# Expert weights in wider column blocks: gate and up pieces of 1024 columns, inner chunks in pairs

## The chip, the cores and the metric

The kernel runs on one core of one Trainium2 chip. The metric is the device time of one execution in microseconds (us). TensorE does the matmuls, VectorE and ScalarE the element-wise work, GpSimd (POOL) some small work and its own transfers, and SyncE (SP) issues the weight transfers.

## The reference

The reference is a two-layer decoder trunk over 256 tokens of width 1024, in float32: a gated linear recurrence with a dense SwiGLU, then sparse attention with a mixture of eight experts of which each token takes two. The part that matters here is the last:

```
def swiglu(xn, w_gu, w_down):
    gate, up = jnp.split(xn @ w_gu, 2, axis=-1)
    return (jax.nn.silu(gate) * up) @ w_down

def moe_swiglu(xn, w_router, w_gu, w_down):
    logits = (xn @ w_router).astype(jnp.float32)
    vals, idx = lax.top_k(logits, TOP_K)
    wts = jax.nn.softmax(vals, axis=-1)
    combine = jnp.sum(jax.nn.one_hot(idx, N_EXPERTS, dtype=jnp.float32) * wts[..., None], axis=-2).astype(xn.dtype)
    out = jnp.zeros_like(xn)
    for e in range(N_EXPERTS):
        out = out + combine[..., e:e + 1] * swiglu(xn, w_gu[e], w_down[e])
    return out
```

Each expert has a gate and up matrix of 1024 x 7168 (3584 columns each) and a down matrix of 3584 x 1024, 42 MB in all.

## The kernel before

The recurrence, the dense layer and the attention come first and are not touched. The expert stage follows, from about 734 us on.

**Routing.** Every expert has up to 128 token rows (one block of 128 is worked on; a second pass is there for an expert with more, behind a test of the largest count). The rows of one expert are fetched from device memory (`x_rows`), transposed on TensorE (`turn_x`, bank 7 of PSUM) and split into a high and a low float32r part, `x_hi` and `x_lo` (`gathered`).

**Pieces.** The weights of an expert come in 42 pieces (`HALVES`) of 1 MB, each a tile of 128 x 2048. SyncE issues a transfer for each (`halves_of`, L472) into a ring of 7 raw slots (`RAWS`), and waits before each until VectorE has worked off the piece that was in the slot (`lo_ready`). ScalarE copies a piece to its high part `w_hi` (L776) and VectorE subtracts that from the raw data to get the low part `w_lo` (L1220). Both parts have 3 buffers (`PARTS`). TensorE gives one back with `w_free` after the last matmul of a piece. `split_to(n)` works the splits off up to piece n in the order of the program, so whatever else ScalarE or VectorE does stands between two splits.

**Products.** `product` (L1681) multiplies one piece with three terms: x_hi by w_hi, x_hi by w_lo, x_lo by w_hi. That is 12 matmuls of 128 x 128 by 512 columns a piece, 504 for an expert. For a gate or up piece (512 rows of the matrix by 512 columns, 2 KB a row) all 12 go to the same PSUM bank: four row blocks by three terms. For a down piece (256 rows by 1024 columns, 4 KB a row) they alternate between banks 5 and 6: two row blocks by three terms by two banks.

**Order.** The inner width of 3584 is cut into 7 chunks (`NCH`) of 512. For chunk c TensorE does the gate product (2 pieces) into bank 0 or 2, turns the hidden tile of chunk c-1 (4 transposes into bank 4, L1697), does the up product (2 pieces) into bank 1 or 3, and then the down product of chunk c-1 (2 pieces). ScalarE takes SiLU of the gate (L800, 128 x 512) when the gate product is done; VectorE multiplies it with the up product (L1270) to `m_h` and tells TensorE with `e_h`; ScalarE and VectorE make `t_hi` (L790) and `t_lo` (L1236) from the transposed tile. Banks, `m_sl`, `m_h`, `t_hi` and `t_lo` have two buffers each, by the parity of c. The order of pieces follows from `gu_item` and `down_item`. At the end of an expert `turn_x` of the next one stands among the last down pieces, ScalarE copies the result to `m_y` (L821, 128 x 1024), and GpSimd stores it.

**Last expert.** It is written out behind the loop. VectorE there also works out the routing shares (`shares`) and adds the results of the earlier experts to the output (`mix`, L1257, four times 128 x 1024).

Of the kernel before, what the change touches and what calls it, by code (L numbers as in the profile page):

```python
# [41 lines left out]
FF, FFE, NE = 2816, 3584, 8  # L42
# [94 lines left out]
def trunk(nc, x, norm_mix, norm_ffn, hgrn_w_in, hgrn_w_out, hgrn_g_norm, kv_norm, kv_w,  # L137
# [3 lines left out]
    with ExitStack() as ctx:  # L141
# [230 lines left out]

        def gu_item(c, half):
            return half if c == 0 else 3 * c - 1 + half

        def down_item(c):
            return 3 * c + 4 if c < NCH - 1 else PER_E - 1

        expert_items = sorted([(gu_item(c, g), "gate up".split()[g], c) for c in range(NCH) for g in range(2)]
                              + [(down_item(c), "down", c) for c in range(NCH)])

        def used(s, E):

            return w_free, E * HALVES + (s + 1 + PARTS)

        def part_of(s, w):

            return w[s % PARTS][:, :].rearrange("p (k c) -> p k c", c=D if expert_items[s // 2][1] == "down" else 512)  # L390

        def split_part(eng, s, E):

# [8 lines left out]
        def _(sp):  # L402
# [53 lines left out]
                load(columns(nsa_w_out[0], c * 512))  # L456
            assert i == I_MOE

            def halves_of(e, E, first, last):

                for s in range(first, last):
                    (_, kind, c), a = expert_items[s // 2], s % 2
                    if not (isinstance(E, int) and HALVES * E + s < RAWS):
                        sp.wait_ge(lo_ready, E * HALVES + (s - RAWS + 1))
                    if kind == "down":
                        src = moe_w_down[0, bass.ds(e, 1), c * 512 + a * 256:c * 512 + (a + 1) * 256, :]
                    else:
                        c0 = (kind == "up") * FFE + c * 512
                        src = moe_w_gu[0, bass.ds(e, 1), 512 * a:512 * a + 512, c0:c0 + 512]
                    src = src.rearrange("o (k p) c -> p (o k) c", p=P)  # L470
                    dst = raw[:, s % RAWS, :].rearrange("p (k c) -> p k c", c=D if kind == "down" else 512)
                    sp.dma_start(dst, src).then_inc(raw_full[s % RAWS], 16)  # L472

            def all_experts(E0):
# [119 lines left out]
        def _(act):  # L594
# [196 lines left out]

            def expert(e, E, q, last=False):
                ahead = 0 if last else PARTS - 1
                for c in range(NCH):
                    s = 2 * gu_item(c, 0) + 1
                    split_to(s + PARTS, E)
                    act.wait_ge(*used(s, E))
                    if c >= 2:
                        act.wait_ge(e_h, E * NCH + (c - 1))
                    act.activation(m_sl[:, c % 2, :], bank[:, 2 * (c % 2), :], ACT.Silu).then_inc(e_sl, 1)  # L800
                    if c:
                        hidden(c - 1, E)
                    if last and not q and c == 2:
                        split_to(2 * gu_item(2, 1) + 1 + PARTS, E)
                        act.wait_ge(PT_ps, 1)
                        act.activation(m_PT[:, :], bank[:, 7, 0:T], ACT.Copy).then_inc(PT_ready, 1)
                split_to(min(2 * gu_item(NCH - 1, 1) + 1 + PARTS, HALVES + ahead), E)
                if not last:
                    gathered(0, E + 1)
                split_to(min(2 * down_item(NCH - 2) + PARTS, HALVES + ahead), E)  # L810
# [34 lines left out]
        def _(dve):  # L845
# [413 lines left out]

            def expert(e, E, q, last=False):  # L1260
                ahead = 0 if last else PARTS - 1
                for c in range(NCH):
                    if c:
                        split_to(2 * gu_item(c, 0) + 1 + PARTS, E)
                        hidden(c - 1, E)
                    s = 2 * gu_item(c, 1) + 1
                    split_to(min(s + PARTS, HALVES + ahead), E)
                    dve.wait_ge(e_sl, E * NCH + (c + 1))
                    dve.wait_ge(*used(s, E))
                    dve.tensor_tensor(m_h[:, c % 2, :], m_sl[:, c % 2, :], bank[:, 2 * (c % 2) + 1, :],  # L1270
                                      ALU.mult).then_inc(e_h, 1)
                    if last and not q:
                        if c == 1:
                            shares()
                        if 2 <= c < 6:
                            tb, j = divmod(c - 2, 2)
                            dve.wait_ge(y_got[tb], 32)
                            step(mix(tb, j, m_mix))
                if not last:
                    gathered(0, E + 1)  # L1280
                split_to(min(2 * down_item(NCH - 2) + PARTS, HALVES + ahead), E)
# [35 lines left out]
        def _(pe):  # L1317
# [368 lines left out]
            def wide(c, up, E):  # L1686

                for a in range(2):
                    ks = range(4 * a, 4 * a + 4)
                    product([bank[:, 2 * (c % 2) + up, :]], 2 * gu_item(c, up) + a, E,  # L1690
                            [x_hi[:, k, :] for k in ks], [x_lo[:, k, :] for k in ks], 512, a == 0, a == 1)

            def turn(c, E):

                pe.wait_ge(e_h, E * NCH + (c + 1))
                for b in range(4):
                    last = tp(bank[:, 4, P * b:P * b + P], m_h[:, c % 2, P * b:P * b + P], ident)  # L1697
                last.then_inc(e_hT_ps, 1)

            def down(c, E, halves=(0, 1)):  # L1700
                pe.wait_ge(t_lo_ok, E * NCH + (c + 1))
                for a in halves:
                    bs = range(2 * a, 2 * a + 2)
                    product([bank[:, 5, :], bank[:, 6, :]], 2 * down_item(c) + a, E,
                            [t_hi[:, c % 2, b, :] for b in bs], [t_lo[:, c % 2, b, :] for b in bs], D,
                            c == 0 and a == 0, c == NCH - 1 and a == 1)

# [7 lines left out]

            def expert(e, E, q, last=False):
                pe.wait_ge(x_lo_ok, E * 2 + 2)
                for c in range(NCH):
                    if c >= 2:
                        pe.wait_ge(e_h, E * NCH + (c - 1))  # L1720
                    wide(c, 0, E)
                    if c:
                        if c > 1:
                            pe.wait_ge(t_lo_ok, E * NCH + (c - 1))
                        turn(c - 1, E)
                    wide(c, 1, E)
                    if c:
                        if c == 1:
                            pe.wait_ge(y_ready, E + (1 + q))
                        if last and not q and c == 2:  # L1730
# [4 lines left out]
                        if c < NCH - 1:  # L1735
                            down(c - 1, E)
# [55 lines left out]
```

## Time and profile before

| | us |
|---|---|
| median of 3 runs | 1725.07 (1723.33 to 1728.29) |
| profiled execution, its own time | 1724.83 |
| its span, first to last instruction | 1723.2 |
| mean granted TensorE clock over the span | 0.951 |
| TensorE busy over the span | 1612.6 (94%) |
| VectorE busy | 1145.4 (66%) |
| ScalarE busy | 934.5 (54%) |
| moved by the DMA engines | 455.56 MB, mean 264 GB/s |

The page cuts the span in 40 slices of 43 us. From slice 18 on, where the experts begin, the slices of TensorE and of the DMA engines are both at nine tenths or more; before that the DMA engines are mostly idle. Matmul ends are modelled, and matmuls overlap in the records: the distance between the starts of two matmuls is what tells their pace. A granted clock of 1.00 is 2.4 GHz, 0.5 is 1.2 GHz.

### The profile page before, as it was taken

The page shows a single profiled execution, that of the slowest core. Times are in us where ns is not written, and L with a number is a line of the kernel's source. Part 1 is how long each engine was busy: PE and PEld are TensorE (multiplying, and loading weights), DVE is VectorE, ACT ScalarE, POOL GpSimd, SP SyncE. Part 2 cuts the span into 40 slices and gives each one's busy share as a digit, 9 for nine tenths or more (in the row PEclk, how much of TensorE's full clock was granted, in tenths as well). Part 3 has the DMA queues.
Part 4 walks back from the last instruction along what each step waited for, and adds up shares of the span by engine and source line. Part 5 has one row for each costly group of instructions (what it writes and reads, how often), then busy time and mean ns, then how long its engine had stood idle before and what let it go on. Part 6 is the DMA issues. An engine that isn't in the chain of part 4 may idle for free.

```text
span 1723.2 us, 20000 instructions
## 1 busy us (share of the span) xinstructions
PE 1612.6 (94%) x7164; PEld 1253.3 (73%) x7164; DVE 1145.4 (66%) x1022; ACT 934.5 (54%) x906; POOL 56.8 (3%) x79
## 2 busy tenths in 40 slices
PE   6998899998976898799999999999999999999997
PEld 5866478876443786578878788788788788788775
DVE  1176245544022365378888888888888888888986
ACT  3323144433000132277777777877877877777774
POOL 2000000000001000100000000000000000000200
PEclk9999899999988578899999999999999999999999
DMA  9633235448464000099999999999999999999993
GB/s 364 218 99 98 69 127 195 171 146 215 157 234 170 1 1 1 28 354 376 353 390 374 349 385 367 364 380 363 370 382 365 366 369 360 383 366 352 399 384 126
DMA packets 212737, 455.56 MB, mean 264 GB/s; under 512 B 9825, under 2 KB 36490, under 8 KB 212682
## 3 DMA queue, kind: packets, MB, share of 16 engines
q1 hardware_dynamic: 206282, 440.97, 71.1%
q0 software_dynamic: 3536, 12.96, 1.9%
q10 hardware_dynamic: 2864, 0.90, 0.2%
q8 instruction: 33, 0.54, 0.1%
q14 instruction: 22, 0.18, 0.0%
HBM read 434.89 MB, written 19.92 MB: 264 GB/s over the span
## 4 chain that ended last, share of the span: by engine, by line
PE 87%; DVE 7%; ACT 2%; issue 2%; POOL 1%; DMA 0%; ACTq 0%; DVEq 0%; POOLq 0%
PE bank L1681 50%; PE bank L1439 11%; PE bank L1421 3%; PE bank L1362 3%; PE bank L1395 3%; PE bank L1489 3%; DVE w_lo L1220 2%; PE bank L1544 2%; PE bank L1384 2%; PE bank L1623 2%; PE bank L1597 1%; PE bank L1697 1%; ACT w_hi L776 1%; PE bank L1513 1%; POOL small L512 1%
## 5 line engine op out<-in xcount | busy, mean ns | idle before, releaser
L1220 DVE TENSOR_TENSOR w_lo<-ring,w_hi 128x2048 fp32r<-128x2048 f32 x336 | 764.2, 2291 | 131.6 <-ACT w_hi L776 131.1
L776 ACT ACTIVATE w_hi<-ring 128x2048 fp32r<-128x2048 f32 x336 | 643.4, 1920 | 181.7 <-PE bank L1681 178.8
L1681 PE MATMUL bank<-w_hi,x_hi 128*128 128x512 f32 x896 | 356.7, 398 | 14.9 <-DVE w_lo L1220 10.4
L1681 PE MATMUL bank<-w_hi,x_lo 128*128 128x512 f32 x896 | 350.4, 391 | 0.0
L1681 PE MATMUL bank<-w_lo,x_hi 128*128 128x512 f32 x896 | 350.2, 391 | 0.0
L1681 PEld LDWEIGHTS bank<-w_hi,x_hi 128*128 128x128 f32 x896 | 168.5, 188 | 55.6 <-DVE w_lo L1220 12.8
L1681 PEld LDWEIGHTS bank<-w_hi,x_lo 128*128 128x128 f32 x896 | 168.6, 188 | 36.8
L1681 PEld LDWEIGHTS bank<-w_lo,x_hi 128*128 128x128 f32 x896 | 168.9, 188 | 33.5
L1681 PE MATMUL bank<-w_hi,t_hi 128*128 128x512 f32 x448 | 143.0, 400 | 0.1
L952 DVE TENSOR_TENSOR ring_lo<-ring,f_whi 128x1024 fp32r<-128x1024 f32 x66 | 80.8, 1226 | 92.6 <-ACT f_whi L677 92.6
L1681 PE MATMUL bank<-w_lo,t_hi 128*128 128x512 f32 x448 | 141.2, 396 | 0.0
L1681 PE MATMUL bank<-w_hi,t_lo 128*128 128x512 f32 x448 | 141.0, 396 | 0.0
L677 ACT ACTIVATE f_whi<-ring 128x1024 fp32r<-128x1024 f32 x66 | 69.7, 1059 | 96.7 <-PE bank L1439 96.7
L1681 PEld LDWEIGHTS bank<-w_hi,t_lo 128*128 128x128 f32 x448 | 84.3, 188 | 20.5
L1681 PEld LDWEIGHTS bank<-w_lo,t_hi 128*128 128x128 f32 x448 | 84.4, 188 | 20.3
L1681 PEld LDWEIGHTS bank<-w_hi,t_hi 128*128 128x128 f32 x448 | 82.4, 188 | 21.3 <-DVE w_lo L1220 3.1
L1439 PE MATMUL bank<-f_whi,f_xhi 128*128 128x512 f32 x176 | 71.6, 407 | 4.2 <-DVE f_xlo L969 4.2
L1439 PE MATMUL bank<-f_whi,f_xlo 128*128 128x512 f32 x176 | 70.8, 402 | 0.0
L1439 PE MATMUL bank<-ring_lo,f_xhi 128*128 128x512 f32 x176 | 69.8, 397 | 0.0
L754 ACT ACTIVATE arena<-bank,small 128x128 f32<-128x128 f32 (+1 forms) x64 | 26.1, 419 | 61.4 <-DVE small L1153 61.4
L1362 PE MATMUL bank<-xT,ring 128*128 128x256 f32 x256 | 57.2, 387 | 2.2 <-DVE xT L861 2.2
L1362 PEld LDWEIGHTS bank<-xT,ring 128*128 128x128 f32 x256 | 49.7, 194 | 9.4 <-DVE xT L861 2.3
(251 smaller groups left out, 1631.1 us busy)
## 6 DMA issues: line engine op xcount, KB each, us to landing
ring<-in_moe_w_gu SPq DMA_DIRECT2D x224, 1024.0 KB, 7.2
ring<-in_moe_w_down SPq DMA_DIRECT2D x112, 1024.0 KB, 7.2
ring<-in_ffn_w_gu SPq DMA_DIRECT2D x22, 1024.0 KB, 6.7
ring<-in_hgrn_w_in SPq DMA_DIRECT2D x16, 1024.0 KB, 14.3
ring<-in_ffn_w_down SPq DMA_DIRECT2D x10, 1024.0 KB, 7.0
x_rows<-arena SPq DMA_DIRECT2D x2, 4096.0 KB, 21.1
ring<-in_kv_w SPq DMA_DIRECT2D x6, 1024.0 KB, 6.4
ring<-in_hgrn_w_out SPq DMA_DIRECT2D x4, 1024.0 KB, 8.1
```

Source lines behind the costliest of these rows:

```text
L677: act.activation(f_whi[d % F_PARTS][:, :], quarter(d)[0], ACT.Copy).then_inc(q_hi, 1)
L776: act.activation(w_hi[s % PARTS][:, :], raw[:, s % RAWS, :], ACT.Copy).then_inc(hi_ready, 1)
L952: dve.tensor_tensor(quarter(d)[1], quarter(d)[0], f_whi[d % F_PARTS][:, :].bitcast(F32), ALU.subtract).then_inc(q_lo, 1)
L1220: dve.tensor_tensor(w_lo[s % PARTS][:, :], raw[:, s % RAWS, :], w_hi[s % PARTS][:, :].bitcast(F32), ALU.subtract).then_inc(lo_ready, 1)
L1362: last = mm(bank[:, j % 4, 256 * hh:256 * hh + 256], cols(i)[:, k, c0:c0 + P], xT[:, k, :], start=k == 0, stop=k == KD - 1)
L1384: last = mm(bank[:, b, P * hh:P * hh + P], (a_kl if m > 1 else a_k)[:, hd, ts], (a_ql if m else a_q)[:, hd, ts], start=True, stop=True)
L1395: last = mm(bank[:, n % 4, :], xT[:, k, P * tb:P * tb + P], cols(4 + it)[:, k, :], start=k == 0, stop=k == KD - 1)
L1421: last = mm(bank[:, b0 + 2 * c + tb, :], lhs[:, k, P * tb:P * tb + P], cols(i0 + c)[:, k, :], start=k == 0, stop=k == KD - 1)
L1439: done = [mm(out_, x_, w_[:, k, 512 * b:512 * b + 512], start=start and n == 0, stop=stop and n == 2) for b, out_ in enumerate(dst)]
L1489: last = mm(bank[:, j % 4, :], b_xk[:, k, P * tb:P * tb + P], cols(I_KV + it)[:, k, :], start=k == 0, stop=k == KD - 1)
L1544: last = mm(bank[:, j, :], xT[:, k, P * tb:P * tb + P], cols(I_Q + it)[:, k, :], start=k == 0, stop=k == KD - 1)
L1681: last = mm(out_, x_[k], w[:, k, 512 * b:512 * b + 512], start=start and k == 0 and n == 0, stop=stop and k == HALF // width - 1 and n == 2)
```

## The change

The gate and up matrices are read in blocks of 1024 columns. The inner width now has four groups C (`WIDE`): three of 1024 columns (two chunks each) and one of 512. In a wide group a gate or up piece is 256 rows by 1024 columns (4 KB a row), so that a group has 4 gate pieces, into banks 0 and 1, and 4 up pieces, into banks 2 and 3. The last group keeps pieces of 512 rows by 512 columns, 2 of gate and 2 of up. The down pieces stay as they are. There are 42 pieces and 504 matmuls an expert, as before.

SiLU and the multiply work on both chunks of a group at once (128 x 1024). The banks and `m_sl`, `m_h` no longer alternate from group to group: a gate product of group C waits for the SiLU of group C-1 (`e_sl`), and the first turn of a group's hidden tiles waits for the multiply (`e_h`). The two chunks are turned between single gate pieces of the next group, and both down products follow its up product. The splits are ordered to match.

```diff
-PER_E = 3 * NCH
-HALVES = 2 * PER_E
+WIDE = 4
+HALVES = 6 * NCH
...
+        def pieces(C):
+            return 4 if C < WIDE - 1 else 2
+        def gate(C, a):
+            return (0, 8, 20, 32)[C] + a % pieces(C)
+        def up(C, a):
+            return gate(C, 0) + pieces(C) + a % pieces(C)
+        def down_half(c, a):
+            return (16, 18, 28, 30, 36, 38, 40)[c] + a
+        narrow = [f(WIDE - 1, a) for f in (gate, up) for a in range(2)]
...  SyncE
+            for C in range(WIDE):
+                n = pieces(C)
+                for a in range(n):
+                    rows, cols = slice(a * D // n, (a + 1) * D // n), slice(D * C, D * C + 256 * n)
+                    sources[gate(C, a)] = (moe_w_gu, rows, cols)
+                    sources[up(C, a)] = (moe_w_gu, rows, slice(FFE + cols.start, FFE + cols.stop))
...  ScalarE
+                for C in range(WIDE):
+                    if C:
+                        split_to(gate(C, 0) + PARTS, E)
+                        hidden(2 * C - 2, E)
+                    if 1 <= C < WIDE - 1:
+                        split_to(gate(C, 2) + PARTS, E)
+                        hidden(2 * C - 1, E)
+                    split_to(gate(C, -1) + PARTS, E)
+                    act.wait_ge(*used(gate(C, -1), E))
+                    if C:
+                        act.wait_ge(e_h, E * WIDE + C)
+                    n = pieces(C) // 2
+                    act.activation(m_sl[:, 0:n, :], bank[:, 0:n, :], ACT.Silu).then_inc(e_sl, 1)
...
+                split_to(up(WIDE - 1, 0) + PARTS, E)
+                hidden(NCH - 2, E)
...  VectorE
+                    split_to(up(C, -1) + PARTS, E)
+                    dve.wait_ge(e_sl, E * WIDE + (C + 1))
+                    dve.wait_ge(*used(up(C, -1), E))
+                    n = pieces(C) // 2
+                    dve.tensor_tensor(m_h[:, 0:n, :], m_sl[:, 0:n, :], bank[:, 2:2 + n, :], ALU.mult).then_inc(e_h, 1)
+                    if adds and C == 0:
+                        shares()
+                    if adds and C == 2:
+                        added(2)
...  TensorE
+            def wide(C, b0, s, a, E):
+                n = pieces(C)
+                ks = range(KD // n * a, KD // n * a + KD // n)
+                product([bank[:, b0 + b, :] for b in range(n // 2)], s, E,
+                        [x_hi[:, k, :] for k in ks], [x_lo[:, k, :] for k in ks], 256 * n, a == 0, a == n - 1)
             def turn(c, E):
-                pe.wait_ge(e_h, E * NCH + (c + 1))
+                pe.wait_ge(e_h, E * WIDE + (c // 2 + 1))
+                if c:
+                    pe.wait_ge(t_lo_ok, E * NCH + c)
...
+                for C in range(WIDE):
+                    if C:
+                        pe.wait_ge(e_sl, E * WIDE + C)
+                    for a in range(pieces(C)):
+                        wide(C, 0, gate(C, a), a, E)
+                        if C and a == 0:
+                            turn(2 * C - 2, E)
+                        if 1 <= C < WIDE - 1 and a == 2:
+                            turn(2 * C - 1, E)
+                    for a in range(pieces(C)):
+                        wide(C, 2, up(C, a), a, E)
+                        if C == WIDE - 1 and a == 0:
+                            turn(2 * C - 1, E)
...
+                    if 1 <= C < WIDE - 1:
+                        down(2 * C - 2, E)
+                        down(2 * C - 1, E)
+                down(NCH - 3, E, (0,))
                 if not last:
                     turn_x(0, E + 1)
+                down(NCH - 3, E, (1,))
                 down(NCH - 2, E, (0,))
                 turn(NCH - 1, E)
```

In the last expert VectorE does `shares` after the multiply of group 0, one addition after each turn's subtraction in group 2, one after its multiply and one at the start of group 3.

## Rows read from the trace of the kernel before

**Rows 1.** Busy time by engine, length of one expert; then clock, DMA share, GB/s.

```profile
core 0: us, PE busy (x) PEld busy (x) DVE busy (x) ACT busy (x) POOL busy (x), PEclk, DMA share, GB/s
...
1101.00:1223.00 122.00, 120.60 (x542) 98.12 (x541) 105.58 (x65) 92.97 (x68) 1.06 (x2) 1.00 1.01 370
```

**Rows 2.** Waits from 760 to 1600 us: total us, times, longest.

```profile
ACT w_hi L776 <- PE bank L1681: 149.3, 202, 1.0
DVE w_lo L1220 <- ACT w_hi L776: 112.1, 174, 3.2
...
PE bank L1681 <- DVE w_lo L1220: 8.1, 6, 1.4
```

**Rows 3.** Waits of SyncE's queue, same stretch.

```profile
SPq L472 <- DVE w_lo L1220: 661.4, 290, 4.9
```

**Rows 4.** The page's DMA issues: count, KB each, us to landing.

```profile
ring<-in_moe_w_gu SPq DMA_DIRECT2D x224, 1024.0 KB, 7.2
ring<-in_moe_w_down SPq DMA_DIRECT2D x112, 1024.0 KB, 7.2
```

**Rows 5.** Timeline of TensorE, a gate product's second piece and the turn behind it.

```profile
1010.55 0.39 PE L1681 MATMUL bank<-w_hi,x_lo 128*128 128x512 f32 x1
...
1013.27 0.40 PE L1681 MATMUL bank<-w_hi,x_lo 128*128 128x512 f32 x1
1013.50 0.60 PE L1697 MATMUL bank<-cf,arena 128*128 128x128 f32 x4
1013.86 0.48 PE L1681 MATMUL bank<-w_hi,x_hi 128*128 128x512 f32 x1
1014.17 0.39 PE L1681 MATMUL bank<-w_lo,x_hi 128*128 128x512 f32 x1
1014.40 0.39 PE L1681 MATMUL bank<-w_hi,x_lo 128*128 128x512 f32 x1
1014.63 0.40 PE L1681 MATMUL bank<-w_hi,x_hi 128*128 128x512 f32 x1
1014.87 0.39 PE L1681 MATMUL bank<-w_lo,x_hi 128*128 128x512 f32 x1
```

**Rows 6.** Timeline of TensorE, a down piece: first row and the thirteenth matmul.

```profile
1002.42 0.62 PE L1681 MATMUL bank<-w_hi,t_hi 128*128 128x512 f32 x2
...
1005.23 0.63 PE L1681 MATMUL bank<-w_hi,t_hi 128*128 128x512 f32 x2
```

**Rows 7.** Timeline, dense layer: gate and up, then down; twelve matmuls apart each.

```profile
270.78 0.39 PE L1439 MATMUL bank<-ring_lo,f_xhi 128*128 128x512 f32 x1
...
273.57 0.39 PE L1439 MATMUL bank<-ring_lo,f_xhi 128*128 128x512 f32 x1
...
396.69 0.63 PE L1439 MATMUL bank<-f_whi,f_hlo 128*128 128x512 f32 x2
...
399.50 0.63 PE L1439 MATMUL bank<-f_whi,f_hlo 128*128 128x512 f32 x2
```

**Rows 8.** Timeline of ScalarE at the start of an expert.

```profile
1222.46 1.03 ACT L821 ACTIVATE arena<-bank 128x1024 f32<-128x1024 f32 x1 [1.24 <-PE bank L1681]
...
1224.80 3.72 ACT L776 ACTIVATE w_hi<-ring 128x2048 fp32r<-128x2048 f32 x2
1228.54 1.28 ACT L800 ACT_TABLE_LOAD   x1
1229.83 0.60 ACT L800 ACTIVATE arena<-bank 128x512 f32<-128x512 f32 x1
```

**Rows 9.** Timeline of VectorE, same place.

```profile
1226.83 4.49 DVE L1220 TENSOR_TENSOR w_lo<-ring,w_hi 128x2048 fp32r<-128x2048 f32 x2 [3.18 <-ACT w_hi L776]
```

**Rows 10.** Instruction groups by line, 760 to 1600 us: busy us, mean ns.

```profile
L1220 DVE TENSOR_TENSOR w_lo<-ring,w_hi 128x2048 fp32r<-128x2048 f32 x291 | 662.6, 2291 | 112.1 <-ACT w_hi L776 112.1
L776 ACT ACTIVATE w_hi<-ring 128x2048 fp32r<-128x2048 f32 x291 | 557.3, 1920 | 149.4 <-PE bank L1681 149.3
...
L1270 DVE TENSOR_TENSOR arena<-arena,bank 128x512 f32<-128x512 f32 x48 | 32.7, 681 | 0.0
```

**Rows 11.** Timeline of TensorE: first matmul of two experts, third piece of the second.

```profile
1100.28 0.39 PE L1681 MATMUL bank<-w_hi,x_hi 128*128 128x512 f32 x1
...
1222.18 0.40 PE L1681 MATMUL bank<-w_hi,x_hi 128*128 128x512 f32 x1
...
1229.17 0.50 PE L1681 MATMUL bank<-w_hi,x_hi 128*128 128x512 f32 x1 [1.35 <-DVE w_lo L1220]
```

**Rows 12.** Timeline of VectorE in the last expert.

```profile
1630.87 1.28 DVE L1257 SCALAR_TENSOR_TENSOR h<-arena,h 128x1024 f32<-128x1024 f32 x1
```

More of the change, by code:

```diff
@@ L371, in left @@
             return res_ps, 8 + 2 * (i - I_OUT) + 2
[L375 to L382, printed above, removed]
+        def pieces(C):
[7 more added lines that the diff above has]
+        narrow = [f(WIDE - 1, a) for f in (gate, up) for a in range(2)]
         def used(s, E):
@@ L457, in _ @@
             assert i == I_MOE
+            sources = {}
+            for C in range(WIDE):
[4 more added lines that the diff above has]
+                    sources[up(C, a)] = (moe_w_gu, rows, slice(FFE + cols.start, FFE + cols.stop))
+            for c in range(NCH):
+                for a in range(2):
+                    sources[down_half(c, a)] = (moe_w_down, slice(512 * c + 256 * a, 512 * c + 256 * a + 256), slice(0, D))
             def halves_of(e, E, first, last):
                 for s in range(first, last):
-                    (_, kind, c), a = expert_items[s // 2], s % 2
+                    w, rows, cols = sources[s]
                     if not (isinstance(E, int) and HALVES * E + s < RAWS):
                         sp.wait_ge(lo_ready, E * HALVES + (s - RAWS + 1))
[L465 to L471, printed above, removed]
+                    src = w[0, bass.ds(e, 1), rows, cols].rearrange("o (k p) c -> p (o k) c", p=P)
+                    dst = raw[:, s % RAWS, :].rearrange("p (k c) -> p k c", c=512 if s in narrow else D)
                     sp.dma_start(dst, src).then_inc(raw_full[s % RAWS], 16)
@@ L793, in expert @@
                 ahead = 0 if last else PARTS - 1
[L794 to L804, printed above, removed]
+                for C in range(WIDE):
[11 more added lines that the diff above has]
+                    act.activation(m_sl[:, 0:n, :], bank[:, 0:n, :], ACT.Silu).then_inc(e_sl, 1)
+                    if last and not q and C == 1:
+                        split_to(up(1, -1) + PARTS, E)
                         act.wait_ge(PT_ps, 1)
                         act.activation(m_PT[:, :], bank[:, 7, 0:T], ACT.Copy).then_inc(PT_ready, 1)
-                split_to(min(2 * gu_item(NCH - 1, 1) + 1 + PARTS, HALVES + ahead), E)
+                split_to(up(WIDE - 1, 0) + PARTS, E)
+                hidden(NCH - 2, E)
+                split_to(down_half(NCH - 3, 0) + PARTS, E)
                 if not last:
                     gathered(0, E + 1)
-                split_to(min(2 * down_item(NCH - 2) + PARTS, HALVES + ahead), E)
+                split_to(down_half(NCH - 2, 0) + PARTS, E)
                 hidden(NCH - 1, E)
@@ L1261, in expert, with added @@
                 ahead = 0 if last else PARTS - 1
[L1262 to L1278, printed above, removed]
+                def added(n):
+                    tb, j = divmod(n, 2)
+                    dve.wait_ge(y_got[tb], 32)
+                    step(mix(tb, j, m_mix))
@@ new lines, in expert @@
+                adds = last and not q
+                for C in range(WIDE):
+                    if C:
+                        split_to(gate(C, 0) + PARTS, E)
+                        hidden(2 * C - 2, E)
+                        if adds and C == 2:
+                            added(0)
+                    if 1 <= C < WIDE - 1:
+                        split_to(gate(C, 2) + PARTS, E)
+                        hidden(2 * C - 1, E)
+                        if adds and C == 2:
+                            added(1)
+                    if C == WIDE - 1:
+                        if adds:
+                            added(3)
+                        split_to(up(C, 0) + PARTS, E)
+                        hidden(2 * C - 1, E)
+                    split_to(up(C, -1) + PARTS, E)
[5 more added lines that the diff above has]
+                        shares()
+                    if adds and C == 2:
+                        added(2)
@@ L1703, in down @@
                     bs = range(2 * a, 2 * a + 2)
-                    product([bank[:, 5, :], bank[:, 6, :]], 2 * down_item(c) + a, E,
+                    product([bank[:, 5, :], bank[:, 6, :]], down_half(c, a), E,
                             [t_hi[:, c % 2, b, :] for b in bs], [t_lo[:, c % 2, b, :] for b in bs], D,
@@ L1717, in expert @@
                 pe.wait_ge(x_lo_ok, E * 2 + 2)
[L1718 to L1730, printed above, removed]
+                for C in range(WIDE):
+                    if C:
+                        pe.wait_ge(e_sl, E * WIDE + C)
[9 more added lines that the diff above has]
+                            turn(2 * C - 1, E)
+                    if C == 1:
+                        if last and not q:
                             pe.wait_ge(PW_ready, 1)
```

14 lines of the change are left out of this document (5 added, 9 removed).

## The prediction

> **What bounds the kernel now.** I read the page's slices first (TensorE and the DMA engines are both full from 740 us to the end), then the busy times of one expert's stretch, the waits, and the timeline of single matmuls. In an expert's 122 us TensorE is busy 120.60 us, DMA share 1.01 at 370 GB/s, VectorE 105.58, ScalarE 92.97 [rows 1]. The waits decide between the two full ones: from 760 to 1600 us TensorE waited 8.1 us, in 6 places, always for a low part `w_lo`; ScalarE's splits waited for matmuls to give back a buffer and VectorE's for ScalarE; no one waited for a weight transfer [rows 2]. The queue that issues the transfers waited 661.4 us for VectorE to free a raw slot [rows 3]. A transfer lands 7.2 us after its issue [rows 4]; its slot's next use is seven pieces away, 7 x 2.72 = 19.0 us less the 4.2 us of a split, so some 7 us are spare. The expert stage is a stream of matmuls that the loads follow.
>
> Now its pace. A piece of weights (1 MB) is 12 matmuls. In a gate piece, all 12 into one bank, the starts lie 13.27 - 10.55 = 2.72 us apart [rows 5]; in a down piece, whose matmuls alternate between banks 5 and 6, 2.81 us [rows 6]. That is 227 against 234 ns a matmul, same shapes, clock 1.00. It is not the stationary tile alone: the dense layer's gate product (bank changed after every 3 matmuls) takes 2.79 for 12 and its down product (two banks in turn) 2.81 [rows 7], with other tiles in other places. Every product here that changes bank inside a piece runs at the slower pace.
>
> **The change part by part.**
>
> Transfers: 24 of an expert's 28 gate and up pieces become 256 rows by 4 KB instead of 512 by 2 KB. Bytes, count (336) and ring stay. Down pieces have 4 KB rows already and land in the same 7.2 us [rows 4], so little is to be had, and it would be hidden: 0.
>
> By the Trainium skill ("DMA: Bandwidth & Descriptors", Where 436 GB/s comes from) HBM binds such loads at about 358 GB/s. The trace's 370 [rows 1] is above that, and by the rule loads, at their ceiling whatever their rows, would set the pace; the waits say no. By it the time would stay near 1725, where case 4 below ends.
>
> Pace: a wide piece is now 2 row blocks x 3 products x 2 banks, the order of a down piece. I take it at 2.81 us: 24 x 0.09 = 2.16 us per expert. Bounds: 0 (pace stays 2.72) and 24 x 0.09. From this goes the settling that old pieces had after a bank change (the row after the transposes shows 0.31, 0.23, 0.23, 0.24 us for the first gaps, not 0.227 [rows 5]): some 0.02 to 0.05 us in 11 places, -0.2.
>
> The Trainium skill ("TensorE: Matmul & The Clock Gate", Back-to-back issue gap) lets the gap depend on the number of columns alone, about 216 ns at 512. The trace shows 227 and 234 at 512 columns, so the rule misses what I price; by it the pace term would be 0, which is case 2 below.
>
> Transposes: still seven turns of 4 an expert, each costing 0.36 us and a slow first gap (13.50 to 13.86, then 0.31) [rows 5]. They only move, from between gate and up to after single pieces: 0.
>
> Fewer, larger operations: per expert 4 SiLUs instead of 7 (three over 1024) and 4 multiplies instead of 7. A 1024-wide copy of ScalarE takes 1.03 [rows 8]. A multiply of 512 takes 0.68, at the rate of the 2048-wide subtraction (2.29) 1024 is about 1.2 [rows 10]. The fixed costs saved lie on engines that wait anyway: 0. But a long operation stands in front of a split. A split is 1.92 + 2.29 [rows 10] with about 0.3 of handing over (the low part starts 0.11 after the high one ends, TensorE 0.05 after it), 4.5 us from the freeing of a buffer, and the piece is due two pieces later: 5.62 us at the new pace, so 1.1 us of slack.
>
> Head of an expert, where the slack goes. Before: the output copy at 1222.46, a table load, then the splits of pieces 2 and 3 at 1224.80, a second table load at 1228.54, SiLU at 1229.83 [rows 8]; the first low part is made at 1226.83 [rows 9] and TensorE, which began the expert at 1222.18, starts piece 2 only at 1229.17 [rows 11]. The copy still stands ahead of split 2, so 1229.17 stays; pieces 0 and 1 are now 0.18 longer inside that wait: -0.18. Then, on the same clock: piece 3 starts at 32.07, 4 at 34.88, and 6 is due at 40.50. The split of 4 runs 28.5 to 30.4 (the table load and SiLU no longer ahead of it), that of 5 needs piece 2 done and ends at 34.2. Now the table load comes (to 35.5), SiLU of 1024 to 36.4, split 6 to 38.4, its low part 38.5 to 40.8: TensorE waits 0.3 us. The multiply of this pair must follow the last up piece (pieces 6 and 7 from 40.8, done at 46.5), but stands behind the low part of piece 9, whose buffer came free at 43.9 and which ends at 48.2; it ends at 49.4. TensorE does piece 8 till 49.3 and then turns, so it waits 0.1 us. Later pairs have down pieces in between for the low parts to catch up: 0. Head and handover: +0.4 - 0.2 = +0.2 us. Unfavourable bound: all six long operations (3 SiLUs, 3 multiplies) each expose 0.5 us, +3.
>
> Waits for single banks: `pe.wait_ge(e_sl)` ahead of a gate product is met one up product (11.2 us) after SiLU's input was ready; queued behind it would be all of TensorE. Banks 2 and 3 are guarded by the turn's `e_h`, bank 4 by the new `t_lo_ok` wait, two pieces (5.6 us) after the earlier turn, whose copy and subtraction take about 2 us: 0.
>
> Last expert: the routing shares (1.9 us of small operations) and four additions of 1.28 us on VectorE [rows 12] stand between subtractions before as after, with the slack of 1.1 us; I count them equal, with -1 as the favourable bound, since two of the additions now follow each other within wide pieces. There the output copy of an expert before is still ahead, so the same +2.2.
>
> Sum: 2.16 - 0.2 + 0.2 = 2.2 us per expert; x 8 = 17.3, less about 1 for the last. Rounded, +16.5. The profiled execution was 1724.8 us with a span of 1723.2, 1.6 us outside it, and the median 1725.07, 0.2 above it. So 1725 + 16.5 = 1741.5 us.
>
> **The rivals.** 0.3% (5.2 us) is about what a measurement of this kernel can tell from no change.
>
> 1. Pace and small waits as above: 1741.5. For it: three products out of three with bank changes are slow. Against: none is an `x_hi` product. Own range 1735 to 1748.
> 2. The pace stays 2.72 (it depends on the stationary tile, or is kept over a pair), but waits come. Pieces then are due earlier (slack 0.9), the head wait becomes 0.6, the handover 0.3 and two smaller of 0.1: about +1 per expert, 1733. For it: the `x` pieces settle to 227 within some matmuls of a disturbance.
> 3. The waits grow: slack is not regained between long operations, +3 us an expert on top of the pace: 1765. It decides once ScalarE and VectorE are over 2.81 us a piece for long. Against: VectorE has 105.58 of 122 us busy [rows 1], 0.4 us spare a piece.
> 4. No change: pace stays and the head's later SiLU is hidden: 1725 within 5. It needs both terms to fail.
> 5. Faster, the other side: the loads are the real pace and longer rows lift them. TensorE can gain no more than what it waits: 8.1 us in this stretch and about 2 beyond, so 1715. It decides if splits wait for data. Against: no such wait is in the trace [rows 2, 3], and the 4 KB transfers land no sooner than the 2 KB ones [rows 4].
>
> **How the numbers follow.** Chances: 0.60, 0.14, 0.10, 0.10, 0.06. The predicted time is that of case 1, 1741.5. The range of 8 in 10 takes in cases 1 and 2 and the near part of 3: 1731 to 1757. Slower by over 0.3% (above 1730): cases 1 and 3 and nearly all of 2, 0.83; within: case 4 and a little of 2, 0.11; faster 0.06.
>
> **What the profile after would show.** Right: wide gate and up pieces 2.80 to 2.82 us from start to start; an expert's first matmuls about 124.1 us apart instead of 121.9 [rows 11]; a wait of TensorE for `w_lo` at an expert's third and seventh piece; the second table load after four splits; fewer and larger packets, landing in 7 us or less, and still no wait for them. Wrong in the pace if the 12 starts stay within 2.72; wrong in the small waits if TensorE's waits for `w_lo` grow far over 2 us an expert, or if ScalarE is seen waiting for a transfer. What would overturn the whole: a matmul pace below 227 ns, which nothing in the trace offers.

## The result and the profile after

The changed kernel takes 1734.6 us (median of 22 runs) against 1724.4 for the kernel before (22 runs); the ratio is 1.0052, 95% interval 1.004 to 1.0064. It is slower by about 9 us by the ratio, 10.3 by the medians: outside 0.3%, and on the forecast side. One run of 1863.3, at a lower granted clock, is among the 22; the ratio leaves it out. The time lies in the range of 1731 to 1757 but beside the predicted 1741.5: it is that of case 2 (1733), whose chance was put at 0.14, and not of case 1.

The page and the views after, from the top. The page's first line, and its DMA part:

```profile
span 1733.7 us, 20010 instructions
...
DMA packets 163585, 455.56 MB, mean 263 GB/s; under 512 B 9825, under 2 KB 36490, under 8 KB 163530
...
ring<-in_moe_w_gu SPq DMA_DIRECT2D x224, 1024.0 KB, 7.3
ring<-in_moe_w_down SPq DMA_DIRECT2D x112, 1024.0 KB, 7.2
```

49,152 packets fewer than the 212,737 of before, and a gate or up piece lands 7.3 us after its issue, not sooner than [rows 4]. The change did what it says to the transfers, and no more came of it.

The same length of one expert as in [rows 1]:

```profile
core 0: us, PE busy (x) PEld busy (x) DVE busy (x) ACT busy (x) POOL busy (x), PEclk, DMA share, GB/s
...
980.00:1102.00 122.00, 120.11 (x538) 97.01 (x536) 103.98 (x61) 91.49 (x64) 1.06 (x2) 1.00 0.98 364
```

The clock is 1.00 as before. Every engine does a little less in 122 us: 538 matmuls instead of 542. How many fall into such a stretch depends on where it begins (536 from 978.8 us on), so the loss is not read from here but from the distance between two experts, below: 1.1%. The waits from 760 to 1600 us, beside [rows 2]:

```profile
ACT w_hi L791 <- PE bank L1718: 127.6, 151, 1.9
DVE w_lo L1241 <- ACT w_hi L791: 120.0, 158, 3.1
ACT t_hi L805 <- PE bank L1736: 59.7, 49, 1.6
...
PE bank L1718 <- DVE w_lo L1241: 10.6, 12, 1.3
```

TensorE waits 12 times for a low part instead of 6. This view counts as idle only what is left after the modelled end of the last matmul, so a stop of 0.3 us does not appear in it; starts show more. Nobody waits for a weight transfer. ScalarE's new 59.7 us is its place in the order: it stands at `t_hi` until a turn is done.

The pace, in TensorE's timeline, from the fourth piece of an expert, a wide gate piece, into the fifth (each row of x2 is two banks):

```profile
993.42 0.62 PE L1718 MATMUL bank<-w_hi,x_hi 128*128 128x512 f32 x2
993.87 0.62 PE L1718 MATMUL bank<-w_lo,x_hi 128*128 128x512 f32 x2
...
996.14 0.62 PE L1718 MATMUL bank<-w_hi,x_hi 128*128 128x512 f32 x2
```

996.14 - 993.42 is 2.72 us for 12 matmuls that change bank every time: the pace of [rows 5], not of [rows 6]. An expert, from its first matmul to the next one's, and the stop at its seventh piece:

```profile
982.21 0.40 PE L1718 MATMUL bank<-w_hi,x_hi 128*128 128x512 f32 x1
...
999.76 0.61 PE L1718 MATMUL bank<-w_hi,x_lo 128*128 128x512 f32 x2
1000.79 0.73 PE L1718 MATMUL bank<-w_hi,x_hi 128*128 128x512 f32 x2 [0.41 <-DVE w_lo L1241]
...
1008.63 0.61 PE L1718 MATMUL bank<-w_hi,x_lo 128*128 128x512 f32 x2
1009.37 0.66 PE L1736 MATMUL bank<-cf,arena 128*128 128x128 f32 x4
...
1105.44 0.63 PE L1718 MATMUL bank<-w_hi,x_hi 128*128 128x512 f32 x2
```

1105.44 - 982.21 is 123.23 us against 121.90 in [rows 11]: +1.33. By a stop I mean, from here on, what the distance between two starts has over that of a running stream. In a running stream the rows of two would follow each other by 0.45; 1.03 at the seventh piece is a stop of 0.58, and 0.74 ahead of the transposes one of 0.29 to 0.34 (the last matmul of a pair, 0.23 after its row, is followed by the transposes at 0.23 when nothing is late). ScalarE in that stretch, beside [rows 8]:

```profile
982.49 1.03 ACT L842 ACTIVATE arena<-bank 128x1024 f32<-128x1024 f32 x1 [1.14 <-PE bank L1718]
983.54 1.28 ACT L791 ACT_TABLE_LOAD   x1
984.83 5.52 ACT L791 ACTIVATE w_hi<-ring 128x2048 fp32r<-128x2048 f32 x3
992.25 1.92 ACT L791 ACTIVATE w_hi<-ring 128x2048 fp32r<-128x2048 f32 x1 [1.90 <-PE bank L1718]
994.19 1.28 ACT L821 ACT_TABLE_LOAD   x1
995.49 1.03 ACT L821 ACTIVATE arena<-bank 128x1024 f32<-128x1024 f32 x1
996.41 3.71 ACT L791 ACTIVATE w_hi<-ring 128x2048 fp32r<-128x2048 f32 x2
```

and VectorE:

```profile
998.45 6.70 DVE L1241 TENSOR_TENSOR w_lo<-ring,w_hi 128x2048 fp32r<-128x2048 f32 x3 [1.85 <-ACT w_hi L791]
1005.89 2.29 DVE L1241 TENSOR_TENSOR w_lo<-ring,w_hi 128x2048 fp32r<-128x2048 f32 x1 [0.75 <-ACT w_hi L791]
1008.10 1.22 DVE L1310 TENSOR_TENSOR arena<-arena,bank 128x1024 f32<-128x1024 f32 x1
```

The table load that stood in the shadow of the head's wait now stands right ahead of SiLU, and both ahead of the split of the seventh piece (996.41), whose low part begins at 998.45 and is ready at 1000.7; TensorE starts at 1000.79. The multiply of the first pair (1.22 us, foreseen 1.2) ends at 1009.32, and the transposes start at 1009.37.

Laid out for one expert, from the matmul starts: stops at the seventh piece 0.58, before the first turn 0.34, at the third up piece of groups 1 and 2 0.12 and 0.15, 1.19 us together. Each of the three at a piece costs 0.13 to 0.18 more, since the distances behind it are 0.335, 0.235, 0.233 us and so on instead of 0.227; with that the stops come to 1.65 us. Against them stands what the old order had and the new one hardly has: slow distances where one product followed another (0.11 us at the fifth piece, 0.03 at each of five later gate products), and 0.12 of a stop at the last piece. That leaves the 1.3. The first expert loses 1.9 us, the last nothing (122.60 us to its last matmul against 122.73). From the first matmul of the stage to the last it is 9.7 us.

### The profile page after: what moved, and what is told of

The parts are those of the page before. It is cut to its first block, busy times and chain, and to the rows that moved or that the text cites. A ratio compares the mean times of both kernels' runs of the same rounds, so it can differ in the third digit from the quotient of the medians.

```text
span 1733.7 us, 20010 instructions
## 1 busy us (share of the span) xinstructions
PE 1621.2 (94%) x7164; PEld 1254.7 (72%) x7164; DVE 1143.7 (66%) x998; ACT 928.5 (54%) x882; POOL 54.4 (3%) x79
## 4 chain that ended last, share of the span: by engine, by line
PE 82%; DVE 8%; ACT 4%; issue 4%; POOL 1%; DMA 0%; DVEq 0%; ACTq 0%; POOLq 0%
PE bank L1718 45%; PE bank L1476 11%; PE bank L1399 3%; PE bank L1458 3%; PE bank L1432 3%; DVE w_lo L1241 3%; ACT w_hi L791 3%; PE bank L1526 3%; PE bank L1581 2%; PE bank L1421 2%; PE bank L1660 1%; PE bank L1736 1%; PE bank L1634 1%; PE bank L1550 1%; POOL small L527 1%
## 5 line engine op out<-in xcount | busy, mean ns | idle before, releaser
L1718 PE MATMUL bank<-w_hi,x_hi 128*128 128x512 f32 x896 | 296.3, 400 | 16.1 <-DVE w_lo L1241 12.0
L1718 PE MATMUL bank<-w_lo,x_hi 128*128 128x512 f32 x896 | 288.3, 391 | 0.0
L1718 PE MATMUL bank<-w_hi,x_lo 128*128 128x512 f32 x896 | 287.9, 391 | 0.0
L1718 PEld LDWEIGHTS bank<-w_hi,x_hi 128*128 128x128 f32 x896 | 163.8, 189 | 59.3 <-DVE w_lo L1241 24.8
L805 ACT ACTIVATE t_hi<-bank 128x512 fp32r<-128x512 f32 x56 | 33.5, 599 | 69.5 <-PE bank L1736 69.5
```

The costliest lines, as they stand in the source:

```text
L1718: last = mm(out_, x_[k], w[:, k, 512 * b:512 * b + 512], start=start and k == 0 and n == 0, stop=stop and k == HALF // width - 1 and n == 2)
```

## The experiments

"An expert" below is always the distance between the first matmuls of the fifth and the sixth expert, which from the second expert to the seventh repeats within 0.12 us in every kernel here. It is a better measure than the median: the expert stage begins between 727 and 735.5 us in kernels that are equal up to there.

**1. Whose pace is it? The stationary tiles change places** (kernel before).

```diff
-        x_hi, x_lo = (over(..., at_xT + 4 * i * KD * P) ...)
-        t_hi, t_lo = (over(..., at_arena + 4 * (ARENA - 2048 + 1024 * i)) ...)
+        x_hi, x_lo = (over(..., at_arena + 4 * (ARENA - 4096 + 1024 * i)) ...)
+        t_hi, t_lo = (over(..., at_xT + 4 * i * KD * P) ...)
```

> The kernel before, with the places of the stationary tiles exchanged: x_hi and x_lo in the area beside the old place of t_hi and t_lo, t_hi and t_lo where x_hi and x_lo were. Nothing else. Theory A (the pace belongs to the place of the stationary tiles): gate and up pieces go from 2.72 to 2.81 us and down pieces from 2.81 to 2.72; per expert 28 x 0.09 - 14 x 0.09, +1.2 us, +10 us in all. Theory B (the pace belongs to the two banks 5 and 6, or to the down product's order): gate stays 2.72, down stays 2.81, time unchanged within 3 us.

Timeline of an up piece and of the two down pieces behind it:

```profile
1263.19 0.40 PE L1681 MATMUL bank<-w_hi,x_hi 128*128 128x512 f32 x1
...
1266.00 0.63 PE L1681 MATMUL bank<-w_hi,t_hi 128*128 128x512 f32 x2
...
1268.76 0.62 PE L1681 MATMUL bank<-w_hi,t_hi 128*128 128x512 f32 x2
...
1271.48 0.39 PE L1681 MATMUL bank<-w_hi,x_hi 128*128 128x512 f32 x1
```

The up piece, which multiplies x as a gate piece does, takes 2.81 us, the second down piece 2.72 (the first, 2.76, still settles). The paces have changed places with the tiles; banks and order were not touched. An expert takes 122.88 us, 1.0 more (28 pieces slower, 14 faster), the one run 1731.3. Theory A holds.

**2. The order of banks in a product** (changed kernel).

```diff
-                for k in range(HALF // width):
-                    for n, (x_, w) in enumerate(((hi, wh), (hi, wl), (lo, wh))):
-                        for b, out_ in enumerate(dst):
+                for b, out_ in enumerate(dst):
+                    for k in range(HALF // width):
+                        for n, (x_, w) in enumerate(((hi, wh), (hi, wl), (lo, wh))):
```

> The changed kernel with the bank loop outermost in the product: within a piece the 6 matmuls of the first bank come first, then the 6 of the second. Theory of the prediction (changing bank at every matmul costs): down pieces fall from 2.81 to about 2.72 to 2.75 us, 14 x 0.07 = 1 us an expert, 8 us in all. Theory that bank changes cost nothing: down pieces stay 2.81, wide pieces stay 2.72, time within 3 us of the changed kernel's.

A down piece whose first six matmuls go to one bank and whose last six to the other:

```profile
1278.62 0.40 PE L1718 MATMUL bank<-w_hi,t_hi 128*128 128x512 f32 x1
...
1281.43 0.40 PE L1718 MATMUL bank<-w_hi,t_hi 128*128 128x512 f32 x1
```

2.81 us, as with alternation; an expert 123.17, one run 1734.9. Changing bank costs nothing here. Together with the first run this takes the prediction's largest term away.

**3. What about the place?** Three kernels move `t_hi` and `t_lo` alone, a fourth shifts the whole area.

```diff
 p_t64:   ... at_arena + 4 * (ARENA - 2048 - 8 + 1024 * i)
 p_tlow:  ... at_arena + 4 * (1272 + 1024 * i)            # m_got moved to the end of the area
 p_tmid:  ... at_arena + 4 * (8600 + 1024 * i)
 p_align: small = sb("small", [P, 520])                   # was 512
```

> The kernel before, with t_hi and t_lo 32 bytes lower in the same area, so that they start at a multiple of 64 bytes (they start 32 past one; x_hi and x_lo start at one). Nothing else. Theory A (a stationary tile that starts off a multiple of 64 bytes costs 7 ns a matmul): down pieces go from 2.81 to 2.72 us, 14 x 0.085 x 8 = 9.5 us faster, about 1715. Theory B (the area matters, or what lies near it): down pieces stay 2.81, no change.

> The kernel before, with 8 more columns in the small tensor ahead of the large area, so that all of that area starts at a multiple of 64 bytes. Theory A: as with the two tiles alone, and the dense layer's 792 matmuls, whose moving or stationary tiles lie in that area, fall from 2.79 to 2.81 for 12 to 2.72, another 4 to 5 us: 1710 to 1712. Theory B: no change from 1725.

> The kernel before, with t_hi and t_lo some 52,000 bytes lower in the same area (byte 167,360 of a partition instead of 219,616; x_hi and x_lo are at 147,584), and the rows fetched at the end in their old place. Nothing else. Theory C (tiles high in a partition are read more slowly): down pieces fall from 2.81 to 2.72 us, an expert from 121.9 to 120.7, about 9 us in all, 1715. Theory D (something else than the address, such as the down product's banks, sets it): no change. The exchange of places has already spoken for the place.

> The kernel before, with t_hi and t_lo at byte 196,672 of a partition, between the place that was tried below and the old one. If the pace falls off somewhere between 167,360 and 211,424 bytes (the slow place of the exchange), this tells on which side 196,672 lies: down pieces of 2.72 us, or of 2.81. No other theory; an estimate of mine is 2.81.

| stationary tile starts at byte | over a multiple of 64 | over a multiple of 512 | 12 matmuls, us |
|---|---|---|---|
| 147,584 (x before; t exchanged) | 0 | 128 | 2.72 |
| 196,672 (p_tmid) | 0 | 64 | 2.75 |
| 219,648 (p_align) | 0 | 0 | 2.79 to 2.80 |
| 167,424 (b_best, below) | 0 | 0 | 2.79 to 2.80 |
| 219,584 (p_t64) | 0 | 448 | 2.80 |
| 167,360 (p_tlow) | 0 | 448 | 2.80 |
| 219,616 (t before) | 32 | 480 | 2.81 |
| 211,424 (x exchanged) | 32 | 480 | 2.81 |

The addresses follow from the layout in the code (the first tensor at byte 16,512 of a partition, the large area at 162,272 before the shift), the times from the starts, as these two of p_tlow and two of p_tmid:

```profile
1264.00 0.40 PE L1682 MATMUL bank<-w_hi,t_hi 128*128 128x512 f32 x1
...
1266.80 0.40 PE L1682 MATMUL bank<-w_hi,t_hi 128*128 128x512 f32 x1
```

```profile
1252.66 0.39 PE L1681 MATMUL bank<-w_hi,t_hi 128*128 128x512 f32 x1
...
1255.40 0.39 PE L1681 MATMUL bank<-w_hi,t_hi 128*128 128x512 f32 x1
```

Theory A of the first two (a start at a multiple of 64 bytes is enough) fell: 0.01 us of the 0.09. Theory C (high addresses are slow) fell too: byte 167,360 is slow and 196,672 nearly quick, against my estimate. The times: p_t64 1724.9 (ratio 1.0002, 0.9989 to 1.0015), p_tlow 1725.2 (1.0007, 0.9993 to 1.0022), p_tmid 1712.0 in one run, an expert 121.15; its stage is 5.4 us shorter than that of the kernel before, and the rest is an early beginning of the stage (727.0 instead of 734.4 us). p_align took 1718.2, ratio 0.9974 (0.9959 to 0.9988), an expert 121.58. Its stage is 2.3 us shorter, and the dense layer's matmuls last 194.3 us from the first to the last against 195.1 to 195.4 in p_t64, p_tlow and p_tmid, not the 4 to 5 us less that were expected; what is left of its gain is not accounted for.

In the table the pace goes with the place within 512 bytes. In all its rows the weight buffers, which are the moving operand, lie 128 past a multiple of 512. So it can't say whether the stationary tile's place counts by itself. The dense layer's gate product in p_align can:

```profile
270.80 0.39 PE L1439 MATMUL bank<-f_whi,f_xlo 128*128 128x512 f32 x1
...
273.55 0.39 PE L1439 MATMUL bank<-f_whi,f_xlo 128*128 128x512 f32 x1
```

That is 2.75 us for 12 instead of the 2.79 of [rows 7]. Its stationary tiles `f_xhi` and `f_xlo` lie below the area, at bytes 139,392 and 147,584, both 128 past a multiple of 512, and did not move; `f_whi`, the moving tile of two matmuls in three, went from 480 past a multiple of 512 to 0 (`ring_lo`, of the third, stayed). So the moving tile's place counts too, and a stationary tile at 128 is not enough for 2.72. Whether each place counts for itself or the distance between the two, at 512 bytes or a larger step, no run here tells.

**4. The rows of the transfers** (changed kernel; the counts that ScalarE and VectorE wait for are doubled to match, not shown).

```diff
-                    sp.dma_start(dst, src).then_inc(raw_full[s % RAWS], 16)
+                    for a in range(2):
+                        if w is moe_w_gu and s not in narrow:
+                            at = slice(512 * a, 512 * a + 512)
+                            sp.dma_start(dst[:, :, at], src[:, :, at]).then_inc(raw_full[s % RAWS], 16)
+                        else:
+                            at = slice(dst.shape[1] // 2 * a, dst.shape[1] // 2 * (a + 1))
+                            sp.dma_start(dst[:, at, :], src[:, at, :]).then_inc(raw_full[s % RAWS], 16)
```

> The changed kernel with its wide gate and up pieces fetched in rows of 2 KB again: every piece as two transfers of 512 KB, for a wide one its two column halves, for the others their row halves (4 KB rows of down stay). Theory that the loads are hidden: time as the changed kernel's 1734.6 within 3 us (ratio to before 1.004 to 1.007), no wait for a transfer. Rival that longer rows bring something, which waits elsewhere hide: slower than 1738, with splits waiting for transfers.

1734.8 us, ratio 1.0065 (1.0046 to 1.0084), an expert 123.2: the changed kernel's time with the old rows of 2 KB in the wide pieces, and with twice as many transfers, since every piece comes in two halves. The halves land in:

```profile
ring<-in_moe_w_gu SPq DMA_DIRECT2D x448, 512.0 KB, 6.1
ring<-in_moe_w_down SPq DMA_DIRECT2D x224, 512.0 KB, 5.8
```

No engine waits for a transfer in this run either. The row length is worth nothing to the time here, because the loads are hidden.

**5. The small waits, one by one** (changed kernel). One SiLU of a single column after the first two splits (a_table); the turns of wide groups one gate piece later (a_turn; the order of the splits is moved to match, and ScalarE makes the second `t_hi` of a group behind the SiLU instead of ahead of it, not shown); SiLU in two halves around a split (a_silu).

```diff
 a_table
+                    if C == 0:
+                        split_to(gate(0, 1) + PARTS, E)
+                        act.activation(small[:, 503:504], cf[:, C_ONE:C_ONE + 1], ACT.Silu)
 a_turn
-                        if C and a == 0:
+                        if C and a == (1 if C < WIDE - 1 else 0):
                             turn(2 * C - 2, E)
-                        if 1 <= C < WIDE - 1 and a == 2:
+                        if 1 <= C < WIDE - 1 and a == 3:
                             turn(2 * C - 1, E)
 a_silu
-                    act.activation(m_sl[:, 0:n, :], bank[:, 0:n, :], ACT.Silu).then_inc(e_sl, 1)
+                    if n == 2:
+                        act.activation(m_sl[:, 0, :], bank[:, 0, :], ACT.Silu)
+                        split_to(gate(C, -1) + 1 + PARTS, E)
+                    act.activation(m_sl[:, n - 1, :], bank[:, n - 1, :], ACT.Silu).then_inc(e_sl, 1)
```

> The changed kernel with one SiLU of a single column put after an expert's first two splits, so that the second table load stands where it stood before the change. Theory (the table load and the 1024-wide SiLU ahead of the split of piece 6 make TensorE wait 0.58 us there): that wait falls to 0.2 us or less, the other waits stay; 0.4 to 0.6 x 8 = 3 to 5 us faster than the changed kernel, about 1730 to 1731. Rival (VectorE's backlog from the head makes the wait): it stays 0.58 and the time stays 1734.6.

> The changed kernel with each wide group's turns one gate piece later (after the second and the fourth). Theory (the first turn of group 1 comes too soon for the 1024-wide multiply): TensorE's 0.34 us ahead of that turn go to 0, an expert takes 0.3 us less, 122.9. Rival (the backlog only moves): the wait comes back at a later piece and an expert stays at 123.2.

> The changed kernel with the SiLU of a wide group in two halves of 512 and one split between them. Theory (the 1024-wide SiLU ahead of a split makes the waits at the third up piece of each wide group, 0.58, 0.12 and 0.15 us): the first falls to 0.1, the other two to 0, an expert takes 0.6 us less, 122.6. Rival: VectorE's order makes them and they stay, 123.2.

| | an expert | runs |
|---|---|---|
| changed kernel | 123.19 | 1734.6 |
| a_table | 122.64 | 1728.9, ratio 1.0028 (1.0012 to 1.0043) |
| a_turn | 122.90 | 1730.2, one run |
| a_silu | 122.19 | 1722.7, one run |
| before | 121.9 | 1724.4 |

In a_table ScalarE's second table load is back where [rows 8] has it, and SiLU starts without one:

```profile
1232.24 1.28 ACT L818 ACT_TABLE_LOAD   x1
1233.54 0.20 ACT L818 ACTIVATE small<-cf 128x1 f32<-128x1 f32 x1
1233.64 1.91 ACT L791 ACTIVATE w_hi<-ring 128x2048 fp32r<-128x2048 f32 x1
...
1238.64 1.03 ACT L824 ACTIVATE arena<-bank 128x1024 f32<-128x1024 f32 x1 [0.80 <-PE bank L1721]
```

The stop at the seventh piece fell from 0.58 to 0.07 us and an expert by 0.5 (the fifth expert is the shortest of this run, the others take 122.71 to 122.77). In a_turn the stop before the first turn is gone and an expert takes 0.3 less; the wait does not come back. In a_silu the stop at the seventh piece is 0.15 and those of groups 1 and 2 are gone: 1.0 us, more than the 0.6 foreseen, because a stop takes its slow distances along (0.13 and 0.18 us for two of them). Its one run is 12 us below the changed kernel's median; 8 of these are the experts', the rest is an early beginning of the stage (730.6 instead of 735.0 us). a_silu's 1.0 and a_turn's 0.3 add up to the whole 1.3 us; the two were not run alone together.

**6. A faster version?** On both kernels: the area on multiples of 64, `t_hi` and `t_lo` low, the third piece split ahead of the output copy, and a one-column SiLU first in an expert; a_best also has the halved SiLU and the later turns. Of the edit only the last two of the four are shown:

```diff
-                ahead = 0 if last else PARTS - 1
+                ahead = 0 if last else PARTS
...
+                act.activation(small[:, 503:504], cf[:, C_ONE:C_ONE + 1], ACT.Silu)
```

> The kernel before, with t_hi and t_lo low, the area at a multiple of 64 bytes, an expert's third piece split ahead of the output copy, and a one-column SiLU first in an expert, so that there is one table load instead of two. Theory: 1.2 us an expert from the pace, 0.8 from the head's wait (1.5 to 0.7), 4.5 us in the dense layer: 119.9 an expert, about 1704. Rival: the head's wait comes back at piece 3 or 4 in full and the gain is 14 us, 1710.

> The changed kernel with the same four edits, and with the SiLU of a wide group in halves around a split and the turns one piece later. Theory (small waits were all that set it back): level with the kernel before so edited, 119.9 an expert, within 3 us of it. Rival: wide groups lose something beyond these waits and it stays 5 us or more behind.

b_best: 1714.8 us, ratio 0.9947 (0.9928 to 0.9967), an expert 120.60. The head of an expert there:

```profile
1218.18 1.92 ACT L777 ACTIVATE w_hi<-ring 128x2048 fp32r<-128x2048 f32 x1 [1.18 <-PE bank L1683]
1220.00 1.01 ACT L823 ACTIVATE arena<-bank 128x1024 f32<-128x1024 f32 x1
1221.03 1.28 ACT L795 ACT_TABLE_LOAD   x1
1222.33 0.20 ACT L795 ACTIVATE small<-cf 128x1 f32<-128x1 f32 x1
1222.43 1.90 ACT L777 ACTIVATE w_hi<-ring 128x2048 fp32r<-128x2048 f32 x1
```

The stop at the head, the beginning of an expert, went from 1.5 us at the third piece to 0.64 at the fourth (the distance between the starts is 0.87). Of the 11 us that are missing to 1704, some 8 are in the expert stage, which is 8.4 us shorter instead of 16: the low place of `t_hi` gave next to no pace (2.79 to 2.80 for 12; 120.60 an expert instead of 119.9), and the first and the last expert won less than the others. The dense layer gave about 1 us instead of 4.5. It is the fastest of the versions with more than one run, 0.5% ahead of the kernel before.

a_best missed: 1727.3, ratio 1.0014 (0.9994 to 1.0034), an expert 122.11, 1.5 behind b_best. Its waits of TensorE from 760 to 1600 us:

```profile
PE bank L1722 <- DVE w_lo L1245: 10.8, 20, 0.6
```

Twenty instead of twelve. The first group's stop is gone, but the third up piece of groups 1 and 2 now starts 0.73 us late each (0.96 from start to start), where a_silu alone had no stop and a_turn alone 0.12 to 0.14. ScalarE, then VectorE, ahead of the third up piece of group 1 in the fifth expert:

```profile
1253.99 0.60 ACT L821 ACTIVATE arena<-bank 128x512 f32<-128x512 f32 x1 [0.88 <-PE bank L1722]
1254.48 1.91 ACT L792 ACTIVATE w_hi<-ring 128x2048 fp32r<-128x2048 f32 x1
1256.29 0.59 ACT L823 ACTIVATE arena<-bank 128x512 f32<-128x512 f32 x1
1256.76 0.61 ACT L806 ACTIVATE t_hi<-bank 128x512 fp32r<-128x512 f32 x1
...
1257.40 0.69 DVE L1261 TENSOR_TENSOR t_lo<-bank,t_hi 128x512 fp32r<-128x512 f32 x1 [1.87 <-ACT t_hi L806]
1258.01 6.68 DVE L1245 TENSOR_TENSOR w_lo<-ring,w_hi 128x2048 fp32r<-128x2048 f32 x3
```

Both edits together put half a SiLU, a split and the other half between the turn and `t_hi`. VectorE, whose order has `t_lo` first, stood idle for 1.87 us; the piece's high part had been ready since 1256.39, its low part begins at 1258.01 and ends at 1260.30, and TensorE starts the piece at 1260.35. So the trace shows what these two stops wait for: the two edits together. Another order was not run, so whether wide groups can be level with the kernel before on that footing is not shown.

## Why the prediction was right and wrong

**The bound was right.** TensorE's stream of matmuls sets the stage, and the loads follow. Rows of 4 KB gave packets but no time, and putting back 2 KB gave the same time. Case 5 did not come. The Trainium skill ("DMA: Bandwidth & Descriptors", Where 436 GB/s comes from) has HBM bind at about 358 GB/s, and derives this as half of a stack's bandwidth, one of two cores' shares. The stage runs at 364 GB/s (370 before) on its one core, with nobody waiting for a transfer, so the measurement decides: that limit does not bind this kernel.

**The step that failed is the pace**: "a wide piece is now 2 row blocks x 3 products x 2 banks, the order of a down piece. I take it at 2.81 us", +2.16 an expert, +17 in all. Measured: 2.72, +0. The three slow products that change bank had a second thing in common: each has one or both of its tiles in the large area. The rival had named the stationary tile. The prediction set that aside because of the dense layer's gate product, which is slow with stationary tiles elsewhere; but there it is the moving tile that lies in the area. The exchange and the bank order tell bank and place apart, and p_align shows the moving tile's part. The -0.2 of settling was about right (0.2 measured). The Trainium skill ("TensorE: Matmul & The Clock Gate", Back-to-back issue gap) has a formula with columns alone, 216 ns at 512, for a single matmul, and about 131 ns for a stream of weight loads and matmuls. That the formula has no term for the bank agrees with these runs. The figures don't agree: the matmuls here lie 227 and 234 ns apart. And there is no term for the place that makes these two.

**The small waits were right in kind and too small.** Foreseen +0.4 for head and handover, "later pairs: 0"; measured 0.58 at the seventh piece (0.3), 0.34 at the first turn (0.1), 0.27 in groups 1 and 2 (0). Most of this follows from the first error: at 2.72 each piece is due 0.09 us earlier than at 2.81, so case 2 had written 0.6, 0.3 and twice 0.1, 1.1 us in all, and 1.19 came. The places and the cause (table load and long SiLU ahead of a split, long multiply ahead of a turn) were shown by a_table, a_silu and a_turn, each of which takes its own wait away. The cost of a stop itself was counted without the slow distances behind it, 0.46 us an expert.

**The rest.** Head: the third piece still starts 7.0 us after the first, as foreseen. `e_sl` and `t_lo_ok`: no wait. The last expert: no difference (122.60 and 122.73), -1 had been allowed. That the time fell in the range, and that the kernel is slower at all as forecast, is luck as far as the main term goes: the two errors have opposite signs, 17 us too much for the pace and some 10 too little for everything else, where the forecast had -1 in all.

## What to carry to other kernels

Before a pace is taken from a neighbouring product, ask what else the neighbours share, and where their tiles lie; one run that exchanges two addresses settles it. In a stream with little slack (here 0.9 us), an operation made twice as long does not cost its length but what it pushes past the slack, and it should stand on the far side of the split that is due next. Longer rows for a transfer are worth trying only where something waits for the transfer.

## What was not expected of the hardware

The start of a stationary tile inside its partition changed TensorE's pace for 512 columns from 227 to 234 ns a matmul, with the same shapes, data types and clock of 1.00: 2.72 us for 12 at byte 147,584, 2.75 at 196,672, 2.79 to 2.81 elsewhere. With the stationary tiles left where they were, moving the moving tile by 32 bytes changed 2.79 to 2.75 in the dense layer. After a stop or a turn the first distance is 312 to 341 ns, and up to ten more of 224 to 240 follow before the stream comes to 227, where the place is a good one; at 219,616 it never does (230 to 239). A shift of 32 bytes for the whole area, eight unused columns in a small tensor, made the kernel 0.26% faster. What the place must be was left open, above.
